# Moving the normed activations by up to 256 bytes within their SBUF tile

## The chip, the cores and the metric

The kernel runs on one core of a Trainium2 chip. The metric is the device time of one execution in microseconds (us). Matmuls run on TensorE (PE; its weight loads are listed apart, as PEld), splits and elementwise work on VectorE (DVE) and ScalarE (ACT), transfers of weights are queued by SyncE (SP), masks are made by GpSimd (POOL).

## The reference

Two transformer blocks over 256 tokens of width 1,024, all in fp32. The first is a mixer (gated delta rule on one half, sliding-window attention on the other) with a SwiGLU FFN; the second is two layers, a short convolution with an FFN and a dilated attention with an FFN. What matters here, cut down:

```python
h = rms_norm(x, norm1_w) * (1.0 + scale1) + shift1      # n = 0
proj = h @ w_in                                         # 11 column blocks, and 16 gate columns
x = x + gate1 * (mixed @ w_out)
h2 = rms_norm(x, norm2_w) * (1.0 + scale2) + shift2     # n = 1
x = x + gate2 * ((silu(h2 @ w_gate) * (h2 @ w_up)) @ w_down)
for i in range(2):                                      # mixers n = 2 and 4, FFNs n = 3 and 5
    h = rms_norm_2(x, mix_norm[i])
    x = x + (short_conv_mixer(h, ...) if i == 0 else dilated_attention_mixer(h, ...))
    h = rms_norm_2(x, ffn_norm[i])
    x = x + swiglu(h, w_gate[i], w_up[i], w_down[i])
```

D_MODEL is 1,024, D_FF 2,816, so that an FFN has eleven blocks of 256 hidden columns.

## The kernel before

**Weights.** They come as 146 blocks of 128 x 2,048 fp32 (1 MB) through a ring of three raw buffers. ACT copies each into a rounded high part (line 585, tiles `w_hi`, `w_hi2`), DVE subtracts it into a low part (line 914, `w_lo`, `w_lo2`). Every product is three matmuls, in this order: high x high, high x low, low x high (the helper `three`, or written out in `gate_up` and `token_rows`). All of them are recorded at line 1474, inside the helper `mm`.

**Normed activations.** Each of the six norms writes its result, split in the same way, into one tile, `h_parts`: the high part, 8 pieces (k) of 256 tokens, 8,192 bytes in each partition, and behind it the low part. `normed(n)` gives the two views for norm n; it starts `H_SHIFT[n]` elements (4 bytes each) into the tile, and `H_ROOM` is the room for it:

```python
H_SHIFT, H_ROOM = (0, 0, 0, 16, 0, 64), 96
h_parts = sb("h_parts", [P, 2 * KD * T + H_ROOM], F32R)
for at in (H_SHIFT[n], H_SHIFT[n] + KD * T)      # in normed(n)
h_hi, h_lo = normed(0)
```

`h_hi` and `h_lo`, the views of norm 0, are used by name in the first mixer, in the column blocks of all mixers and in the writes of norm 1. In the first mixer they hold both the projections' input and later the mixed rows, which four `row_block` calls multiply by `w_out`.

**Places.** Tiles lie one after another in each partition. Between `h_parts` and the weights' tiles before it (`w_hi`, `w_lo`, `x_res`, `norm_tmp`) there are only whole multiples of 256 bytes, and `o_hi`, `o_lo`, `w_hi2`, `w_lo2` lie at the same remainder of 256 too. So at shift 0 all operands of a product start at the weights' remainder; pieces and halves inside them are multiples of 512 bytes on. Shift 16 is 64 bytes further, shift 32 is 128, shift 64 is 256.

**Who moves.** In the FFNs (`gate_up`, n = 1, 3, 5) 128 tokens of h are the stationary operand and gate and up weights, 512 columns, move. Per block j and token half t there are 24 such matmuls; then four transposes of the hidden rows (`turn_hid`, line 1977), their copy to `o_hi` by ACT (line 791) and the split by DVE (line 1347), and 24 matmuls of the down product (`token_rows`) of the block before. Nothing else differs between the three FFNs but the weights, some small products for the modulation and spread rows, and the scale of the norm. In the mixers (`column_half`, `column_block`, `row_block`) 128 columns of the weight are stationary and h moves, 256 tokens wide. The exception is the value block of the dilated attention, where tokens of h are stationary and 256 weight columns move. A product for the gates of the first mixer has only 16 weight columns, 64 bytes per k, as its stationary operand.

**Order.** Each engine's program is one list in a fixed order, tied by semaphores that count (`h_hi_ready`, `h_lo_ready`, `block_used`, `hi_ready`, `lo_ready`); no wait looks at an address.

Of the kernel before, what the change touches and what calls it, by code (L numbers as in the profile page):

```python
# [7 lines left out]
ALU, ACT, AX = mybir.AluOpType, mybir.ActivationFunctionType, mybir.AxisListType  # L8
# [15 lines left out]


WARM_NORM1 = 6
H_SHIFT, H_ROOM = (0, 0, 0, 16, 0, 64), 96
NEXP = 6


# [266 lines left out]
def build(nc, stream, x_in, consts_in, vectors_in, gab_in, t5_onehot, t5_log, rel_bias, out):  # L297
    t5_scratch = nc.dram_tensor("t5_scratch", (16, 384), F32, kind="Internal")
    with ExitStack() as ctx:
        s = Semaphores(lambda name: ctx.enter_context(nc.semaphore(name)))  # L300
# [3 lines left out]
        def sb(name, shape, dt=F32, stack=ctx):  # L304
            return stack.enter_context(nc.sbuf_tensor(name, shape, dt))
# [6 lines left out]
        nt = sb("norm_tmp", [P, KD, T])  # L312
# [20 lines left out]
        def normed(n):  # L333

            return [h_parts[:, at:at + KD * T].rearrange("p (k t) -> p k t", k=KD) for at in (H_SHIFT[n], H_SHIFT[n] + KD * T)]

        h_hi, h_lo = normed(0)
# [100 lines left out]
        def big(name):  # L438
            return BIGB[BIG_INDEX[name] % 3]

        norm_scale = [a1[:, :], a2[:, :], vecs("mix0"), vecs("ffn0"), vecs("mix1"), vecs("ffn1"), vecs("final")]
        shift2 = mods[:, 24:32]
# [121 lines left out]
        def _(act):  # L564
# [38 lines left out]
            def h_high(n, ks=range(KD)):  # L603
                for k in ks:
                    act.wait_ge(s.t_ready, 8 * n + k + 1)
                    if n:
                        act.activation(h_hi[:, k, :], nt[:, k, :], ACT.Identity, bias=shift2[:, k:k + 1]).then_inc(s.h_hi_ready, 1)
                    else:
                        act.activation(h_hi[:, k, :], nt[:, k, :], ACT.Copy).then_inc(s.h_hi_ready, 1)


            act.wait_ge(s.vectors_loaded, 16)
# [14 lines left out]
            for q in range(4):  # L627
                act.activation(high_of(0)[:, 2 * q:2 * q + 2, :], raw_of(r)[:, 2 * q:2 * q + 2, :], ACT.Copy).then_inc(s.first_hi, 1)
                if q == 1:
                    mod_rows_copy(0, 1)  # L630
            hi(1)
            h_high(0, range(4))
            act.dma_start(consts[:, N_FIRST:], consts_in[:, N_FIRST:]).then_inc(s.masks_loaded, 16)
            act.wait_ge(s.gab_loaded, 16)
            act.activation(gab_wh[:, :], gab_w[:, :], ACT.Copy).then_inc(s.gab_hi, 1)
            mod_rows_copy(1, 0)
            mod_rows_copy(1, 1)
            h_high(0, range(4, KD))


# [176 lines left out]
            def ffn(f, following):  # L817

                if f:
                    act.wait_ge(s.rms_ready, 2 * f + 2)  # L820
                else:
                    squares(1)
                    root(1)
                    h_high(1)
# [78 lines left out]
        def _(dve):  # L903
# [74 lines left out]
            def h_parts_2():  # L978
                dve.wait_ge(s.rstd_ready, 2)
                rstd = B[3][:, 256:512]  # L980

                def scaled(k):
                    dve.scalar_tensor_tensor(out=nt[:, k, :], in0=x[:, k, :], scalar=a2[:, k:k + 1],
                                             in1=rstd, op0=ALU.mult, op1=ALU.mult).then_inc(s.t_ready, 1)

                def low(k):
                    dve.wait_ge(s.h_hi_ready, 8 + k + 1)
                    dve.scalar_tensor_tensor(out=h_lo[:, k, :], in0=nt[:, k, :], scalar=shift2[:, k:k + 1],
                                             in1=h_hi[:, k, :], op0=ALU.add, op1=ALU.subtract).then_inc(s.h_lo_ready, 1)

                for k in range(KD):
                    scaled(k)
                    if k >= 1:
                        low(k - 1)
                low(KD - 1)
# [52 lines left out]
            for w in range(6):  # L1048
# [6 lines left out]
                if w < 6:  # L1055
# [9 lines left out]
                    for tap in range(1, 4):  # L1065
                        for mt in range(2):
# [4 lines left out]
                                                           in1=o, op0=ALU.mult, op1=ALU.add)  # L1071
# [6 lines left out]
                if w == 1:  # L1078
# [8 lines left out]
                                             op0=ALU.mult, op1=ALU.min).then_inc(s.gate_dve, 1)  # L1087
                if w == 2:
# [9 lines left out]
                                                  op0=ALU.max, op1=ALU.add))  # L1098
                    dve.scalar_tensor_tensor(out=v8(g[:, :]), in0=v8(gt[:, 6, :]), scalar=-1.0,
                                             in1=gt[:, 4, 0:8].unsqueeze(1).broadcast_to([P, TT, 8]),  # L1100
                                             op0=ALU.mult, op1=ALU.mult).then_inc(s.gate_done, 1)
# [79 lines left out]
            for gi in range(4):  # L1181
# [6 lines left out]
                                                    op0=ALU.mult, op1=ALU.mult))  # L1188
            for i, name in enumerate(("sq01", "sq23")):
                wait_big(name)  # L1190
                big_read(name, dve.scalar_tensor_tensor(out=qs[:, 2 * i:2 * i + 2, :], in0=qs[:, 2 * i:2 * i + 2, :],
                                                        scalar=qk_w[:, :], in1=two(big(name)), op0=ALU.mult, op1=ALU.mult))
# [187 lines left out]
            for i in range(4):  # L1380
# [14 lines left out]
                for tap in range(3):  # L1395
                    for mt in range(2):
# [5 lines left out]
                        else:  # L1402
                            link(dve.scalar_tensor_tensor(out=yb[:, mt, :], in0=cu[:, mt, tap:tap + T], scalar=vec[:, ck:ck + 1],
                                                          in1=yb[:, mt, :], op0=ALU.mult, op1=ALU.add))
# [805 lines left out]
```

## Time and profile before

| | |
|---|---|
| median of 3 runs | 1070.27 us (1069.92 to 1070.87) |
| the profiled execution | 1070.55 us, its span 1068.8 us |
| PE busy | 1033.9 us, 97% |
| DVE busy | 618.6 us, 58% |
| ACT busy | 481.0 us, 45% |
| mean granted TensorE clock | 0.981 |

Busy time is the union of the instructions' recorded times. Matmuls are pipelined, so the recorded time of one (some 390 ns for 512 columns) is longer than the distance to the next; the distance comes from start times in the timeline. A timeline row with `x2` is two instructions of one kind in a row, and its time is that of both. What lies outside the span (1.75 us) is not in the trace.

### The profile page before, as it was taken

The page shows a single profiled execution, that of the slowest core. Times are in us where ns is not written, and L with a number is a line of the kernel's source. Part 1 is how long each engine was busy: PE and PEld are TensorE (multiplying, and loading weights), DVE is VectorE, ACT ScalarE, POOL GpSimd, SP SyncE. Part 2 cuts the span into 40 slices and gives each one's busy share as a digit, 9 for nine tenths or more (in the row PEclk, how much of TensorE's full clock was granted, in tenths as well). Part 3 has the DMA queues.
Part 4 walks back from the last instruction along what each step waited for, and adds up shares of the span by engine and source line. Part 5 has one row for each costly group of instructions (what it writes and reads, how often), then busy time and mean ns, then how long its engine had stood idle before and what let it go on. Part 6 is the DMA issues. An engine that isn't in the chain of part 4 may idle for free.

```text
span 1068.8 us, 14676 instructions
## 1 busy us (share of the span) xinstructions
PE 1033.9 (97%) x6224; PEld 898.3 (84%) x6224; DVE 618.6 (58%) x753; ACT 481.0 (45%) x644; POOL 49.5 (5%) x43
## 2 busy tenths in 40 slices
PE   6999979999999999999999999999999999999997
PEld 3799979989788788889987888888899978888885
DVE  1586575866646553568765545454677555454543
ACT  2475443523634434453426434344555465344342
POOL 0000353400000000000000000000000000000000
PEclk9999987989999999999999999999999999999998
DMA  9645004463856653536545364554453326554621
GB/s 346 255 166 184 1 2 158 156 238 131 293 207 236 236 215 140 207 109 237 197 158 191 132 229 155 199 186 175 172 178 119 119 99 215 199 197 157 235 80 39
DMA packets 31552, 185.63 MB, mean 174 GB/s; under 512 B 3008, under 2 KB 5504, under 8 KB 10752
## 3 DMA queue, kind: packets, MB, share of 16 engines
q1 hardware_dynamic: 29952, 180.37, 46.9%
q0 software_dynamic: 832, 3.17, 0.9%
q8 instruction: 49, 0.80, 0.3%
q10 hardware_dynamic: 704, 1.17, 0.3%
q14 instruction: 15, 0.12, 0.0%
HBM read 183.62 MB, written 1.07 MB: 173 GB/s over the span
## 4 chain that ended last, share of the span: by engine, by line
PE 85%; DVE 6%; ACT 4%; DMA 3%; issue 2%; POOL 0%; SPq 0%; ACTq 0%; DVEq 0%; POOLq 0%
PE bank L1474 44%; PE acc L1474 37%; DVE w_lo L914 2%; ACT w_hi L585 2%; DMA raw<-stream 2%; PE bank L1977 1%; DMA AT<-stream 1%; ACT norm_tmp L713 1%; PE bank L1871 1%; DVE soft L1207 1%; PE bank L1817 0%; DVE XT L1183 0%; DVE norm_tmp L1200 0%; PE acc L1567 0%; ACT L786 0%
## 5 line engine op out<-in xcount | busy, mean ns | idle before, releaser
L914 DVE TENSOR_TENSOR w_lo<-raw,w_hi 128x2048 fp32r<-128x2048 f32 x145 | 331.7, 2304 | 162.0 <-ACT w_hi L585 161.8
L1474 PE MATMUL bank<-w_hi,h_parts 128*128 128x512 f32 x1056 | 336.8, 393 | 3.4 <-DVE w_lo L914 3.4
L585 ACT ACTIVATE w_hi<-raw 128x2048 fp32r<-128x2048 f32 x145 | 272.9, 1908 | 98.2 <-PE acc L1474 63.2
L1474 PEld LDWEIGHTS bank<-w_hi,h_parts 128*128 128x128 f32 x1056 | 198.9, 188 | 48.6 <-DVE w_lo L914 4.7
L1474 PE MATMUL bank<-w_lo,h_parts 128*128 128x512 f32 x528 | 207.0, 392 | 0.0
L1474 PE MATMUL acc<-h_parts,w_hi 128*128 128x256 f32 x928 | 173.7, 289 | 0.0
L1474 PEld LDWEIGHTS acc<-h_parts,w_hi 128*128 128x128 f32 x928 | 147.5, 196 | 2.6 <-issue 2.1
L1474 PE MATMUL acc<-h_parts,w_lo 128*128 128x256 f32 x464 | 132.7, 286 | 0.0
L1474 PE MATMUL acc<-w_hi,o_hi 128*128 128x512 f32 x296 | 119.0, 402 | 0.0
L1474 PEld LDWEIGHTS bank<-w_lo,h_parts 128*128 128x128 f32 x528 | 99.5, 188 | 21.1
L1474 PE MATMUL acc<-w_hi,o_lo 128*128 128x512 f32 x296 | 115.7, 391 | 0.0
L1474 PE MATMUL acc<-w_lo,o_hi 128*128 128x512 f32 x296 | 115.6, 391 | 0.0
L1474 PEld LDWEIGHTS acc<-h_parts,w_lo 128*128 128x128 f32 x464 | 90.7, 195 | 0.0
L786 ACT ACTIVATE silu_and_hid<-bank,rms 128x256 f32<-128x256 f32 x44 | 20.9, 476 | 107.3 <-PE bank L1474 107.2
L1347 DVE TENSOR_TENSOR o_lo<-bank,o_hi 128x512 fp32r<-128x512 f32 x33 | 22.8, 692 | 79.7 <-ACT o_hi L791 79.4
L1474 PEld LDWEIGHTS acc<-w_hi,o_lo 128*128 128x128 f32 x296 | 55.6, 188 | 12.3
L1474 PEld LDWEIGHTS acc<-w_hi,o_hi 128*128 128x128 f32 x296 | 55.6, 188 | 11.1 <-issue 0.2
L1474 PEld LDWEIGHTS acc<-w_lo,o_hi 128*128 128x128 f32 x296 | 55.7, 188 | 10.7
L791 ACT ACTIVATE o_hi<-bank 128x512 fp32r<-128x512 f32 x33 | 19.8, 599 | 77.6 <-PE bank L1977 77.6
L1339 DVE SCALAR_TENSOR_TENSOR silu_and_hid<-bank,rms,silu_and_hid 128x256 f32<-128x256 f32 x44 | 21.2, 481 | 34.4 <-ACT silu_and_hid L786 34.4
L550 POOL TENSOR_TENSOR inv_b<-AT,consts 128x512 f32<-128x512 f32 x24 | 35.4, 1502 | 34.2 <-PE bank L1474 34.2
L1474 PE MATMUL bank<-h_parts,w_hi 128*128 128x256 f32 x192 | 34.9, 284 | 0.0
(324 smaller groups left out, 1093.9 us busy)
## 6 DMA issues: line engine op xcount, KB each, us to landing
raw<-stream SPq DMA_DIRECT2D x162, 1024.0 KB, 5.0
AT<-stream SPq DMA_DIRECT2D x2, 1024.0 KB, 11.2
qkT<-stream SPq DMA_DIRECT2D x2, 1024.0 KB, 9.3
X_inv<-stream SPq DMA_DIRECT2D x2, 1024.0 KB, 10.0
keys_queries<-stream SPq DMA_DIRECT2D x2, 1024.0 KB, 10.5
t_tables<-t_scratch POOLq DMA_DIRECT2D x1, 2048.0 KB, 11.8
x_res<-x_in SPq DMA_DIRECT2D x2, 512.0 KB, 5.3
t_tables<-t_scratch POOLq DMA_DIRECT2D x1, 1024.0 KB, 14.1
```

The costliest lines, as they stand in the source:

```text
L550: pool.tensor_tensor(Bm[:, gi, :].rearrange("p (i c) -> p i c", i=4), AT[:, gi, :].rearrange("p (i c) -> p i c", i=4), level_mask[l].unsqu ...
L585: act.activation(high_of(w), raw_of(r), ACT.Copy).then_inc(s.hi_ready, 1)
L713: act.activation(sc[:, hh, c0:c1], sc[:, hh, c0:c1], ACT.Exp, bias=soft[:, 1, 2 * hh + part:2 * hh + part + 1], accum_out=soft[:, 2, 2 * h ...
L786: act.activation(sg[:, T * t:T * t + T], B[t][:, 0:256], ACT.Silu, scale=rms[:, t:t + 1] if f else 1.0).then_inc(s.silu_ready, 1)
L791: act.activation(hid_parts(j)[0].rearrange("p a b -> p (a b)"), B[2][:, :], ACT.Copy).then_inc(s.hid_hi_ready, 1)
L914: dve.tensor_tensor(low_of(w), raw_of(weight_load(w)), high_of(w), ALU.subtract).then_inc(s.lo_ready, 1)
L1207: link(dve.tensor_reduce(soft[:, 0, 2 * hh + part:2 * hh + part + 1], sc[:, hh, c0:c1], AX.X, ALU.max))
L1339: dve.scalar_tensor_tensor(out=o, in0=up, scalar=rms[:, t:t + 1], in1=gate, op0=ALU.mult, op1=ALU.mult).then_inc(s.hid_ready, 1)
L1347: dve.tensor_tensor(low.rearrange("p a b -> p (a b)"), B[2][:, :], high.rearrange("p a b -> p (a b)"), ALU.subtract).then_inc(s.hid_lo_rea ...
L1474: return pe.matmul(o, l, r, start=start, stop=stop, skip_group_check=True)
L1871: ins = pe.transpose(B[gi][:, c], X[:, gi, c], ident)
L1977: ins = pe.transpose(B[2][:, T * i + P * t:T * i + P * t + P], hid[:, T * t + P * i:T * t + P * i + P], ident)
```

## The change

The shifts of the six norms go from (0, 0, 0, 16, 0, 64) elements to (32, 0, 32, 0, 32, 0). The FFNs' h (n = 1, 3, 5) then starts at the weights' remainder, the mixers' h (n = 0, 2, 4) 128 bytes on. Since `h_hi` and `h_lo` stay the views of norm 0, they move with the mixers, and the writes of norm 1 are given the views of their own norm.

```diff
-H_SHIFT, H_ROOM = (0, 0, 0, 16, 0, 64), 96
+H_SHIFT, H_ROOM = (32, 0, 32, 0, 32, 0), 96
...
                     if n:
-                        act.activation(h_hi[:, k, :], nt[:, k, :], ACT.Identity, bias=shift2[:, k:k + 1]).then_inc(s.h_hi_ready, 1)
+                        act.activation(normed(n)[0][:, k, :], nt[:, k, :], ACT.Identity, bias=shift2[:, k:k + 1]).then_inc(s.h_hi_ready, 1)
                     else:
-                        act.activation(h_hi[:, k, :], nt[:, k, :], ACT.Copy).then_inc(s.h_hi_ready, 1)
+                        act.activation(normed(n)[0][:, k, :], nt[:, k, :], ACT.Copy).then_inc(s.h_hi_ready, 1)
...
                     dve.wait_ge(s.h_hi_ready, 8 + k + 1)
-                    dve.scalar_tensor_tensor(out=h_lo[:, k, :], in0=nt[:, k, :], scalar=shift2[:, k:k + 1],
-                                             in1=h_hi[:, k, :], op0=ALU.add, op1=ALU.subtract).then_inc(s.h_lo_ready, 1)
+                    dve.scalar_tensor_tensor(out=normed(1)[1][:, k, :], in0=nt[:, k, :], scalar=shift2[:, k:k + 1],
+                                             in1=normed(1)[0][:, k, :], op0=ALU.add, op1=ALU.subtract).then_inc(s.h_lo_ready, 1)
```

## Rows read from the trace of the kernel before

**Rows 1.** The page: busy time of each engine, and the chain that ended last by line.

```profile
PE 1033.9 (97%) x6224; PEld 898.3 (84%) x6224; DVE 618.6 (58%) x753; ACT 481.0 (45%) x644; POOL 49.5 (5%) x43
...
PE bank L1474 44%; PE acc L1474 37%; DVE w_lo L914 2%; ACT w_hi L585 2%; DMA raw<-stream 2%; PE bank L1977 1%; DMA AT<-stream 1%; ACT norm_tmp L713 1%; PE bank L1871 1%; DVE soft L1207 1%; PE bank L1817 0%; DVE XT L1183 0%; DVE norm_tmp L1200 0%; PE acc L1567 0%; ACT L786 0%
```

**Rows 2.** The list of the tile h_parts: duration min/median/max in ns, first and last start.

```profile
L1474 PE MATMUL bank<-w_hi,h_parts x1056: 387/389/628, 269.3 to 1047.0; 128*128 128x512 f32 x176
...
L1474 PE MATMUL acc<-h_parts,w_hi x928: 277/283/580, 34.1 to 831.9; 128*128 128x256 f32 x186
...
L1474 PE MATMUL bank<-h_parts,w_hi x192: 277/283/363, 465.5 to 519.4; 128*128 128x256 f32 x192
...
L1474 PE MATMUL acc<-w_hi,h_parts x128: 279/283/286, 764.6 to 837.8; 128*128 128x256 f32 x128
...
L810 ACT ACTIVATE h_parts<-bank,vec x16: 465/476/485, 464.0 to 868.6; 128x256 fp32r<-128x256 f32 x16
```

**Rows 3.** Timeline of PE, second FFN, a gate/up product: start us, us, instruction.

```profile
598.95 0.63 PE L1474 MATMUL bank<-w_hi,h_parts 128*128 128x512 f32 x2
...
601.05 0.63 PE L1474 MATMUL bank<-w_hi,h_parts 128*128 128x512 f32 x2
```

**Rows 4.** Timeline of PE, third FFN, a gate/up product.

```profile
920.66 0.62 PE L1474 MATMUL bank<-w_hi,h_parts 128*128 128x512 f32 x2
...
922.70 0.62 PE L1474 MATMUL bank<-w_hi,h_parts 128*128 128x512 f32 x2
```

**Rows 5.** Timeline of ACT, second FFN: line 791 in its third and eighth block.

```profile
605.37 0.60 ACT L791 ACTIVATE o_hi<-bank 128x512 fp32r<-128x512 f32 x1 [2.71 <-PE bank L1977]
...
691.18 0.60 ACT L791 ACTIVATE o_hi<-bank 128x512 fp32r<-128x512 f32 x1 [2.71 <-PE bank L1977]
```

**Rows 6.** Timeline of ACT, third FFN: line 791 in the same two blocks.

```profile
914.23 0.60 ACT L791 ACTIVATE o_hi<-bank 128x512 fp32r<-128x512 f32 x1 [2.68 <-PE bank L1977]
...
998.30 0.60 ACT L791 ACTIVATE o_hi<-bank 128x512 fp32r<-128x512 f32 x1 [2.68 <-PE bank L1977]
```

**Rows 7.** Timeline of PE, first FFN, behind an interruption.

```profile
290.82 0.63 PE L1474 MATMUL bank<-w_hi,h_parts 128*128 128x512 f32 x2
...
292.90 0.62 PE L1474 MATMUL bank<-w_hi,h_parts 128*128 128x512 f32 x2
...
294.94 0.39 PE L1474 MATMUL bank<-w_hi,h_parts 128*128 128x512 f32 x1
```

**Rows 8.** Windows: second FFN, third FFN, conv mixer; busy us (count), PEclk, DMA share, GB/s.

```profile
605.00:691.00 86.00, 86.00 (x385) 69.79 (x383) 41.80 (x30) 35.42 (x30) 0.00 (x0) 1.00 0.51 184
914.00:998.00 84.00, 84.00 (x382) 69.46 (x381) 41.78 (x30) 35.37 (x30) 0.00 (x0) 1.00 0.52 187
464.00:548.00 84.00, 83.27 (x646) 80.82 (x645) 64.34 (x75) 36.47 (x38) 0.00 (x0) 1.00 0.50 174
```

**Rows 9.** Timeline of PE, conv mixer, a column product.

```profile
480.03 0.40 PE L1474 MATMUL bank<-h_parts,w_hi 128*128 128x256 f32 x2
...
481.83 0.40 PE L1474 MATMUL bank<-h_parts,w_hi 128*128 128x256 f32 x2
```

**Rows 10.** Timeline of PE, first projections, behind a restart at 56.12 us.

```profile
56.46 0.28 PE L1474 MATMUL acc<-h_parts,w_lo 128*128 128x256 f32 x1
...
57.90 0.28 PE L1474 MATMUL acc<-h_parts,w_lo 128*128 128x256 f32 x1
```

**Rows 11.** Timeline of PE, the gate product of 16 weight columns.

```profile
49.62 0.39 PE L1474 MATMUL bank<-h_parts,gab_wh 128*16 128x256 f32 x2
...
51.66 0.39 PE L1474 MATMUL bank<-h_parts,gab_wh 128*16 128x256 f32 x2
```

**Rows 12.** Timeline of PE, attention, around an idle stretch.

```profile
770.28 0.28 PE L1474 MATMUL acc<-w_hi,h_parts 128*128 128x256 f32 x1
772.53 2.63 PE L1474 MATMUL bank<-x_res 64*128 64x256 f32 x16 [1.97 <-DVE x_res L1437]
```

**Rows 13.** Window right behind that stretch; columns as in Rows 8.

```profile
773.00:776.00 3.00, 3.00 (x20) 2.75 (x17) 2.37 (x2) 2.08 (x4) 0.00 (x0) 0.51 0.98 371
```

## The prediction

> **What bounds the kernel now.** I read the page first: the matmuls are busy 97% of the span, and the chain that ended last is 85% PE, with line 1474, the one through which nearly every product goes, at 44% and 37% [rows 1]. DVE and ACT are at 58% and 45%. So the pace at which PE starts its matmuls sets the time. The second view, the list of the tile that the change moves, says how many of them read it [rows 2]. Its rows with the high weight hold two of every three products, so the total is one and a half times the count: 1,056 x 1.5 = 1,584 matmuls with 512 columns in the three FFNs (there h is the stationary operand), (928 + 192) x 1.5 = 1,680 with 256 columns where h is the moving one, and 128 x 1.5 = 192 more, in the value blocks of the attention, where h is stationary again and a weight of 256 columns moves. Busy times are no pace, because matmuls overlap; I took paces from start times in the timeline.
>
> **The pace by the place of h.** The three FFNs run the same code. Before, h stands at shift 0 in the first, 64 bytes on in the second, 256 bytes on in the third. The reader should count nine matmuls in each timeline: in the second FFN from 598.95 to 601.05 us, 2.10 us or 233.3 ns each [rows 3]; in the third from 920.66 to 922.70, 2.04 us or 226.7 ns each [rows 4]. The copy of the turned hidden rows (line 791) comes once per FFN block and gives the whole block: (691.18 - 605.37) / 5 = 17.16 us in the second [rows 5], (998.30 - 914.23) / 5 = 16.81 in the third [rows 6]. The first FFN, at shift 0, settles at the third's pace, nine in 292.90 to 294.94 us or 226.7 ns each [rows 7]. So 256 bytes further is no different from none, and 64 bytes further costs 0.35 us per block. 48 gate/up matmuls by 6.6 ns are 0.32 of it; the remaining 0.03 is the start of the down product, which leaves the slow rhythm after a few matmuls.
>
> **The change, part by part.** (1) Third FFN, from 256 bytes to 0: the same remainder, so nothing (first FFN against third above). (2) First FFN: stays at 0. Its writes go through another name, with the same address. (3) Second FFN, from 64 bytes to 0: its eleven blocks should go at the third's pace, 11 x 0.348 = **-3.8 us**. Nothing else holds them: the third FFN does the same loads and splits at that pace, with DVE busy 41.8 of 84 us and DMA at 0.52 [rows 8]. (4) The writes of h: ACT's take 465 to 485 ns over all the places that h has now [rows 2], and DVE's follow them, so nothing. (5) Waits: none is added or taken away, the semaphores and every instruction's place in its queue stay. (6) The three mixers, from 0 to 128 bytes: this is the unknown. They start a matmul every 120.0 ns: fifteen from 480.03 to 481.83 us [rows 9]. That is the conv mixer; the first projections show the same, twelve from 56.46 to 57.90 us [rows 10]. No row has a full 128-column weight load against a 256-column moving operand half a period away.
>
> **The bounds of part 6.** Below: the gate products load only 16 columns, from an operand whose remainder goes on by 64 bytes with each k, and start every 113.3 ns, eighteen in 49.62 to 51.66 us, with no difference between the k [rows 11]. So 113.3 is what 256 moving columns reach here when hardly any weight load runs beside them. The 120.0 is one step of 6.7 ns over that, and the FFN's 64 bytes are one step of the same size. One step down over 1,680 + 192 = 1,872 matmuls is at most -12.5 us; I allow a tenth for places where PE waits for others, so -11.3. Above: one step up, as the 64 bytes did, 1,872 x 6.7 = +12.5 us, with nothing to hide it because PE is already the bound (83.3 of 84 us in the conv mixer [rows 8]). Which value? After an interruption the two streams of PE, loads and matmuls, stand to each other in another way before they settle. In the FFN that costs visibly: nine matmuls from 290.82 to 292.90 take 2.08 us, 231 ns each, before the 226.7 [rows 7]. In the projections the twelve of rows 10 are the ones right behind a restart (at 56.12 us), and they already take 120.0 each on average. So with 256 columns the pace hardly depends on how the two streams stand to each other, at 512 it does. That is nearest to no change, and I take **0** for part 6, with both ends kept.
>
> The Trainium skill (SBUF — State Buffer, "Who interferes with whom") gives TensorE two independent read ports, one for the moving operand and one for the weight load, and says that PE never waits on anyone. By that rule no shift would matter and the sum would be 0, that is 1070.3 us; the 17.16 against 16.81 us per block speaks against it.
>
> The skill also gives a start-to-start time of N / 2.4 GHz + about 2.5 ns for warm bf16 matmuls (TensorE: Matmul & The Clock Gate, "Wait — 56ns, not 53.3ns?"): 109.2 ns for 256 columns. By that the mixers would have 10.8 ns each to give back, an estimated 20 us over 1,872; no row here reaches it.
>
> **The sum.** The profiled execution took 1070.55 us, 1068.8 of it span; the median of the runs is 1070.27, 0.3 less. 1070.55 - 3.8 = 1066.7, and against the median **1066.5**.
>
> **The rivals.**
> *Mixers faster.* If half a period keeps the two streams apart, the pace goes one step down, to 113.3. For it: the step exists [rows 11]. Against: 113.3 is seen only with a load an eighth as long, and a load of 128 columns may need the rest whatever its address. Time: 1070.3 - 3.8 - 11.3 = 1055.
> *Mixers slower (the other side).* The moving stream of one matmul and the load for the next both begin at the same time; at equal remainders they are in step, and an offset made them collide more once, in the second FFN. If 128 bytes do the same as 64, every mixer matmul takes 126.7. For it: the only shifted stage of before is the slow one. Against: there the offset was 64, on the other operand, with 512 columns; and the restarts of the mixers show no slower phase. Time: 1070.3 - 3.8 + 12.5 = 1079. It decides from 3.8 / 1,872 = 2.1 ns per matmul on: above that the kernel is slower than before.
> *Nothing changes.* The second FFN's slower blocks would have to come from something other than the address. Its ACT and DVE work is the same as the third's (35.4 and 41.8 us in five blocks [rows 8]), so little speaks for it. Time: 1070.3.
> *The clock.* PE stands idle for 1.97 us before 772.53 us in the attention [rows 12], and the granted clock is 0.51 from 773 to 776 us, the lower of its two levels; earlier starts could move such a stretch over more or less work [rows 13]. That is 1 to 2 us either way, no case of its own.
>
> **How the numbers follow.** Chances: second FFN gains and the mixers keep their pace (to within about 1 ns) 0.45, with its own range 1065 to 1068.1; mixers faster 0.27; mixers slower 0.23; nothing changes 0.05. About 0.2% (2.1 us) is what a measurement can tell from no change, so "faster" begins at 1068.1. Faster: 0.43 + 0.27 = 0.70. Same: 0.02 of the first case, 0.05 of nothing, 0.03 of mixers slightly slower = 0.10. Slower: 0.20. The range goes from 1054, just past the faster rival, to 1073, which takes in mixers slower by up to 3.5 ns; what lies outside is most of the slower rival and a few hundredths below.
>
> **What would show it.** In the profile after: line 791 of the second FFN every 16.81 us instead of 17.16 (part 3); the first and third FFN unchanged at 16.8 (parts 1, 2); three column matmuls of the conv mixer in 0.36 us (part 6 at 0), 0.34 (faster) or 0.38 (slower), and the length of that stage, 84 us, with it. The prediction is wrong if the mixers' pace moves by over 1 ns per matmul, since there are 1,872 of them, or if the second FFN keeps 17.16.

## The result, and the profile after

The changed kernel takes 1060.22 us (median of 9 runs, 1057.87 to 1062.30), the one before, in runs beside it and the three shown above, 1066.44 us. The ratio is 0.9937, 95% interval 0.9914 to 0.9959: faster, by 6.7 us (4.4 to 9.2). One execution of the kernel before took 3542.74 us, as one of e3_mix_only did later with 4737.13; both are left out of the ratios. The 6.7 us lean on the three runs of before shown above (1069.92 to 1070.87): against the other five, which average 1064.7 us, the changed kernel's average of 1060.1 is 4.7 us less. Two later series of the same kernel against the one before gave 0.9949 (0.9928 to 0.9971) and 0.9944 (0.9924 to 0.9964), 5.4 and 6.0 us. Forecast were 3.8 us.

The page after, the lines that answer to [rows 1]; the picture is the same, PE 97% busy and 84% of the chain:

```profile
PE 1023.1 (97%) x6224; PEld 892.2 (84%) x6224; DVE 618.4 (58%) x753; ACT 480.7 (45%) x644; POOL 49.1 (5%) x43
...
PE bank L1474 44%; PE acc L1474 36%; DVE w_lo L914 2%; ACT w_hi L585 2%; DMA raw<-stream 2%; PE bank L1977 1%; DMA AT<-stream 1%; ACT norm_tmp L713 1%; PE bank L1871 1%; DVE soft L1207 1%; PE bank L1817 0%; DVE XT L1183 0%; DVE h_parts L1318 0%; DVE norm_tmp L1200 0%; ACT L786 0%
```

Line 791 in the second FFN after, the blocks of [rows 5] (timeline of ACT):

```profile
599.31 0.60 ACT L791 ACTIVATE o_hi<-bank 128x512 fp32r<-128x512 f32 x1 [2.68 <-PE bank L1977]
...
683.38 0.60 ACT L791 ACTIVATE o_hi<-bank 128x512 fp32r<-128x512 f32 x1 [2.68 <-PE bank L1977]
```

(683.38 - 599.31) / 5 = 16.81 us per block instead of 17.16, and the third FFN has (988.94 - 904.87) / 5 = 16.81 as before:

```profile
904.87 0.60 ACT L791 ACTIVATE o_hi<-bank 128x512 fp32r<-128x512 f32 x1 [2.68 <-PE bank L1977]
...
988.94 0.60 ACT L791 ACTIVATE o_hi<-bank 128x512 fp32r<-128x512 f32 x1 [2.68 <-PE bank L1977]
```

Nine gate/up matmuls of the second FFN, as in [rows 3], take 2.04 us, 226.7 ns each instead of 233.3 (timeline of PE):

```profile
593.00 0.62 PE L1474 MATMUL bank<-w_hi,h_parts 128*128 128x512 f32 x2
...
595.04 0.62 PE L1474 MATMUL bank<-w_hi,h_parts 128*128 128x512 f32 x2
```

The mixers, where h now moves 128 bytes off. Paces below are worked out from rows rounded to 0.01 us, so that two of them over 33 matmuls that differ by 0.3 ns can be one and the same, and where a range is given it is of averages over 24 matmuls. In the first projections 33 matmuls lie between these two rows (timeline of PE), 3.91 us or 118.5 ns each, where [rows 10] had 120.0:

```profile
63.90 0.40 PE L1474 MATMUL acc<-h_parts,w_hi 128*128 128x256 f32 x2
...
67.81 0.40 PE L1474 MATMUL acc<-h_parts,w_hi 128*128 128x256 f32 x2
```

In the conv mixer of the same execution 30 matmuls take 3.59 us, 119.7 ns each, near the 120.0 of [rows 9]:

```profile
479.99 0.40 PE L1474 MATMUL acc<-h_parts,w_hi 128*128 128x256 f32 x2
...
483.58 0.40 PE L1474 MATMUL acc<-h_parts,w_hi 128*128 128x256 f32 x2
```

The gate product of [rows 11], with its load of 16 columns, went the other way: 18 matmuls take 2.10 us, 116.7 ns each instead of 113.3.

```profile
44.78 0.39 PE L1474 MATMUL bank<-h_parts,gab_wh 128*16 128x256 f32 x2
...
46.88 0.40 PE L1474 MATMUL bank<-h_parts,gab_wh 128*16 128x256 f32 x2
```

**Where the two profiled executions differ.** The spans are 1068.8 and 1059.2 us, 9.6 apart, more than the ratio says. Line 657, ACT's first copy of a projection, shows why (its list: duration, first and last start). First before, then after:

```profile
L657 ACT ACTIVATE inv_p<-acc x6: 580/598/602, 49.5 to 80.6; 128x512 f32<-128x512 f32 x6
```

```profile
L657 ACT ACTIVATE inv_p<-acc x6: 577/602/603, 45.0 to 76.1; 128x512 f32<-128x512 f32 x6
```

The kernel's start is 4.5 us shorter after, though the change has no hold on it: only 74 matmuls that read h are recorded ahead of that copy, 0.1 us at 1.5 ns each. The timeline of PE says it. Before, three matmuls of 256 columns are 0.64 us apart (34.06 to 34.70), the pace of the lower clock level, and 0.35 from 35.89 on:

```profile
34.06 0.63 PE L1474 MATMUL acc<-h_parts,w_hi 128*128 128x256 f32 x2
...
34.70 0.63 PE L1474 MATMUL acc<-h_parts,w_hi 128*128 128x256 f32 x2
...
35.89 0.40 PE L1474 MATMUL acc<-h_parts,w_hi 128*128 128x256 f32 x2
...
36.24 0.40 PE L1474 MATMUL acc<-h_parts,w_hi 128*128 128x256 f32 x2
```

After, they are at the fast pace from the first (31.09 to 31.45), because the clock had risen before they began:

```profile
31.09 0.40 PE L1474 MATMUL acc<-h_parts,w_hi 128*128 128x256 f32 x2
...
31.45 0.40 PE L1474 MATMUL acc<-h_parts,w_hi 128*128 128x256 f32 x2
```

That is a matter of the execution, not of the kernel: e4_scan and e5_mix64 below are the same program up to there, with h of norm 0 at the same 64 bytes, and have the copy at 44.5 and 49.3 us. Among the later profiles three began late as well (line 657 first at 49.5 us in e2_ffn_only, 49.3 in e5_mix64, 49.2 in e8_scan2), the others had it at 44.4 to 47.1. The three runs of before from which the prediction started (1070.27 us) lie at the upper end of what this kernel does: its median was 1064.8 to 1066.0 in three later series of 14 to 21 runs, from 1063.4 to 1070.7. I therefore compare stretches behind the start-up: the first projections (line 657's first copy to line 696), the conv mixer (line 791's last in the first FFN to its first in the second), the second FFN (its first 791 to its last), and the attention (to the third FFN's first). All in us:

| kernel | shifts of mixers, FFNs (bytes) | projections | conv mixer | second FFN | attention |
|---|---|---|---|---|---|
| before | 0; 0, 64, 256 | 73.85 | 123.38 | 163.25 | 146.09 |
| e2_ffn_only | 0; 0 | 73.86 | 123.26 | 159.99 | 146.11 |
| e3_mix_only | 128; 0, 64, 256 | 73.39 | 122.62 | 163.26 | 145.38 |
| after | 128; 0 | 73.48 | 123.25 | 159.99 | 145.57 |
| e1_after | 128; 0 | 73.49 | 122.54 | 159.99 | 145.43 |
| e12_after_again | 128; 0 | 73.39 | 122.51 | 159.99 | 145.39 |
| e5_mix64 | 64; 0 | 72.93 | 121.75 | 159.95 | 142.77 |
| e10_mix176 | 176; 0 | 73.63 | 122.90 | 159.99 | 145.60 |
| e6_mix192 | 192; 0 | 71.52 | 121.99 | 159.95 | 141.54 |
| e11_mix192_again | 192; 0 | 71.51 | 122.00 | 159.99 | 143.18 |
| e9_mix208 | 208; 0 | 73.49 | 121.56 | 159.99 | 145.22 |

### The profile page after: what moved, and what is told of

It reads as the page before. It is cut to its first block, busy times and chain, and to the rows that moved or that the text cites. A ratio compares the mean times of both kernels' runs of the same rounds, so it can differ in the third digit from the quotient of the medians.

```text
span 1059.2 us, 14676 instructions
## 1 busy us (share of the span) xinstructions
PE 1023.1 (97%) x6224; PEld 892.2 (84%) x6224; DVE 618.4 (58%) x753; ACT 480.7 (45%) x644; POOL 49.1 (5%) x43
## 4 chain that ended last, share of the span: by engine, by line
PE 84%; DVE 7%; ACT 4%; DMA 3%; issue 2%; POOL 0%; SPq 0%; ACTq 0%; DVEq 0%; POOLq 0%
PE bank L1474 44%; PE acc L1474 36%; DVE w_lo L914 2%; ACT w_hi L585 2%; DMA raw<-stream 2%; PE bank L1977 1%; DMA AT<-stream 1%; ACT norm_tmp L713 1%; PE bank L1871 1%; DVE soft L1207 1%; PE bank L1817 0%; DVE XT L1183 0%; DVE h_parts L1318 0%; DVE norm_tmp L1200 0%; ACT L786 0%
## 5 line engine op out<-in xcount | busy, mean ns | idle before, releaser
L1474 PEld LDWEIGHTS acc<-h_parts,w_hi 128*128 128x128 f32 x928 | 145.0, 192 | 3.8 <-issue 3.4
L1474 PE MATMUL acc<-w_hi,o_hi 128*128 128x512 f32 x296 | 119.0, 402 | 0.0
```

What stands on the lines that cost most here:

```text
L1474: return pe.matmul(o, l, r, start=start, stop=stop, skip_group_check=True)
```

## The experiments

### The changed kernel twice more

No edit. Beside it ran the two kernels that follow.

> The changed kernel once more, five rounds against the kernel before on one chip. Theory A (the address alone, in the second FFN 0.348 us for each of eleven blocks, in the first projections and the attention about 1 ns per matmul): 4 to 5 us less than before, ratio 0.9955 to 0.9965. Rival B (the first result is all of it, something beyond the matmul paces gives 2 to 3 us more): 6.5 us less, ratio 0.994. Rival C (the moment at which the clock first rises in the start-up differs from run to run, and makes 4 to 5 us of spread in both kernels alike): the ratio goes toward A's, and the profile shows the first fast matmuls at a place of its own, between about 23 and 36 us.

Measured: 1060.97 us, ratio 0.9949 (0.9928 to 0.9971), with the sums of its stretches at -0.36, -0.84, -3.26 and -0.66 against before. The start-up account (C) and the stage account (A) hold together. The interval does not exclude 0.994, so B is not refuted by the ratio; but the stretches behind the start leave 2 to 3 us more no place. Line 657 comes first at 45.6 us here, an early start like that of the first profile.

> The changed kernel again. The sum of the stages in the traces so far is 3.4 us from the second FFN and 1.4 to 2.1 from the mixers: 4.8 to 5.5 us less than before, ratio 0.9948 to 0.9955. The conv mixer at 118.7 or at 120.0 ns.

Measured: 1060.66 us, ratio 0.9944 (0.9924 to 0.9964), which takes in the forecast 0.9948 to 0.9955; the conv mixer at 118.8 ns: 33 matmuls in 3.92 us (timeline of PE).

```profile
479.83 0.40 PE L1474 MATMUL bank<-h_parts,w_hi 128*128 128x256 f32 x2
...
483.75 0.40 PE L1474 MATMUL acc<-h_parts,w_hi 128*128 128x256 f32 x2
```

So the conv mixer of the same kernel has 118.5 and 118.8 ns in two profiles and 119.7 in the first, with 0.7 us between the stretches (123.25 against 122.54 and 122.51). The same place gives one of two rhythms. They also come in one execution: in the attention of the changed kernel most matmuls are at 118.6 ns, but those from 767 to 777 us are at 120.0.

### Only the FFNs, only the mixers

```diff
-H_SHIFT, H_ROOM = (32, 0, 32, 0, 32, 0), 96
+H_SHIFT, H_ROOM = (0, 0, 0, 0, 0, 0), 96
```

> Only the FFN part of the change: all six norms at shift 0, mixers as before. Theory A: line 791 of the second FFN every 16.81 us, mixers at 120.0 ns as before, 3.8 us less than before in all (ratio 0.9964). If the mixers' 128 bytes are worth more than 1 us, this one stays behind the changed kernel by that much; if 128 bytes cost something, it is faster than the changed kernel.

Measured: 1061.22 us, ratio 0.9955 (0.9934 to 0.9976). Line 791 of the second FFN comes at (688.88 - 604.80) / 5 = 16.82 us, and no mixer stretch moves by over 0.12 us against before:

```profile
604.80 0.60 ACT L791 ACTIVATE o_hi<-bank 128x512 fp32r<-128x512 f32 x1 [2.68 <-PE bank L1977]
...
688.88 0.60 ACT L791 ACTIVATE o_hi<-bank 128x512 fp32r<-128x512 f32 x1 [2.68 <-PE bank L1977]
```

The second FFN gives 163.25 - 159.99 = 3.26 us, its first product, which lies in the stretch before, 0.12: 3.4 us in all. The ratio alone can't part the FFN from the mixers: this kernel's interval overlaps those of both later series of the changed kernel. The stretches can.

```diff
-H_SHIFT, H_ROOM = (32, 0, 32, 0, 32, 0), 96
+H_SHIFT, H_ROOM = (32, 0, 32, 16, 32, 64), 96
```

> Only the mixer part: norms 0, 2, 4 at 128 bytes, the second FFN still at 64 and the third at 256 bytes. Theory A: line 791 of the second FFN stays at 17.16 us; first projections at about 118.7 ns per matmul instead of 120.0, conv mixer 120.0; 0.5 to 1.5 us less than before, hardly to be told from no change (ratio 0.9985 to 0.9995). Rival B: 2 to 3 us less (ratio 0.9975).

Measured: 1063.57 us, ratio 0.9975 (0.9959 to 0.9990). The second FFN stays at (685.02 - 599.21) / 5 = 17.16:

```profile
599.21 0.60 ACT L791 ACTIVATE o_hi<-bank 128x512 fp32r<-128x512 f32 x1 [2.71 <-PE bank L1977]
...
685.02 0.60 ACT L791 ACTIVATE o_hi<-bank 128x512 fp32r<-128x512 f32 x1 [2.71 <-PE bank L1977]
```

The interval lies below 1, but part of that may be the start-up, since none of these runs is among the late ones of 1066 to 1071 us that the kernel before has. The stretches show what the 128 bytes of the mixers are worth by themselves, in the conv mixer too, which was expected to stay at 120.0 ns: 0.46 in the projections, 0.76 in the conv mixer, 0.71 in the attention, 1.9 us together, and 0.3 behind the projections, where the clock also moves. With the FFN's 3.4 that makes 5.3 to 5.7, beside the 5.4 and 6.0 that the two later series of the changed kernel gave.

### Other places of h

To give each norm a place of its own, the column products of the second and third mixer, and the value block of the third, read their own norm's views:

```diff
-H_SHIFT, H_ROOM = (32, 0, 32, 0, 32, 0), 96
+H_SHIFT, H_ROOM = (16, 32, 48, 48, 8, 8), 96
...
-                    ins = three(bank[:, 256 * mt:256 * mt + 256], wh[:, k, c], wl[:, k, c], h_hi[:, k, :], h_lo[:, k, :],
+                    ins = three(bank[:, 256 * mt:256 * mt + 256], wh[:, k, c], wl[:, k, c], normed(views)[0][:, k, :], normed(views)[1][:, k, :],
```

> A look at six other places of h: norm 0 at 64 bytes, norm 2 at 192, norm 4 at 32 (h moves, 256 columns), norm 1 at 128, norm 3 at 192, norm 5 at 32 (h stationary, 512 columns move). If the cost goes in steps of 6.7 ns with the distance in bytes modulo 256, the FFN paces are 226.7, 233.3 or 240 ns and FFN blocks 16.8, 17.16 or 17.5 us. If only equal remainders are good, all three FFNs are at 17.1 us or above. If h moving with 256 columns is indifferent, the mixers stay between 118 and 121 ns at all three places.

Measured: 1062.37 us, one run, like those of the next two kernels. The moving h had 117.8 ns at 64 bytes (projections) and at 192 (conv mixer) and mostly 116.7 to 118.2 at 32 (attention): it is not indifferent. Stationary, in the second FFN at 192 bytes, 12 matmuls take 2.74 us, 228.3 ns each, and in the third at 32 bytes 12 take 2.80, 233.3 (timelines of PE):

```profile
592.09 0.62 PE L1474 MATMUL bank<-w_hi,h_parts 128*128 128x512 f32 x2
...
594.83 0.62 PE L1474 MATMUL bank<-w_hi,h_parts 128*128 128x512 f32 x2
```

```profile
896.65 0.63 PE L1474 MATMUL bank<-w_hi,h_parts 128*128 128x512 f32 x2
...
899.45 0.63 PE L1474 MATMUL bank<-w_hi,h_parts 128*128 128x512 f32 x2
```

> A second look at six places of h: norm 0 at 96 bytes, norm 2 at 160, norm 4 at 224 (moving), norm 1 at 16, norm 3 at 224, norm 5 at 160 (stationary). From the first look: h stationary at 0 has 226.7 ns, at 32, 64, 128 and 192 bytes 233.8, 233.4, 232.2 and 229. If the distance counts by itself and grows gently toward 256 again, 224 bytes is near 227 to 228, 160 near 230 to 231, and 16 between 226.7 and 233.8. For h moving 117 to 118.7 everywhere off 0, so that only equal remainders (120.0) are the poor case.

The edit was the same with (24, 4, 40, 56, 56, 40). Measured: 1071.76 us, in an execution whose start was late. The forecast for h moving fell at 96 bytes, where the projections have 120.0 ns, as at 0 (33 matmuls in 3.96 us; timeline of PE):

```profile
63.23 0.40 PE L1474 MATMUL acc<-h_parts,w_hi 128*128 128x256 f32 x2
...
67.19 0.40 PE L1474 MATMUL acc<-h_parts,w_hi 128*128 128x256 f32 x2
```

At 160 bytes the conv mixer has 117.2 to 118.8 ns, at 224 the attention's column products have 117.8 to 118.7. The FFN block per place of the stationary h, from line 791 in these two profiles and those above:

| bytes off the weights' remainder | 0 | 16 | 32 | 64 | 128 | 160 | 192 | 224 |
|---|---|---|---|---|---|---|---|---|
| us per FFN block | 16.81 | 16.80 | 17.14 | 17.16 | 17.07 | 17.18 | 16.92 | 17.14 |

Not a gentle function of the distance: 224 bytes, which I had expected near 227 ns, is as bad as 32 (17.14), while 192 is nearly good. Neither "steps of 6.7 ns" nor "only equal remainders are good" describes it; 0 is the best place for the stationary h, shared by 16. The entries for 16 and 128 bytes rest on two blocks each: they are the first FFN's, most of whose blocks are longer for other reasons (17.2 us and more at 0 too).

### One common move of all operands

```diff
-        sb("spacer_before", [P, 24])
+        sb("spacer_before", [P, 32])
```

> The changed kernel with the spacer before the weights' tiles 128 instead of 96 bytes: all places relative to each other stay, the weights' own remainder of 256 goes from 224 to 0. Theory A (only the distance between stationary and moving operand counts): paces as in the changed kernel, 226.7 ns in the FFNs, 118.6 to 120.0 in the mixers, 113.3 for the gate product. Rival (the 6.7 ns over 106.7 of the gate product are those of an operand that doesn't start at a multiple of 64 bytes, one more line to read): one step less everywhere, 220, 112 to 113 and 107 to 109 ns, which over all matmuls would be 20 us.

Measured: 1062.73 us. The weights' tiles, h and everything behind them move by 32 bytes, the raw blocks don't. 226.7 ns in the FFN (15 matmuls in 3.40 us) and 118.8 in the projections (33 in 3.92), where the changed kernel had 226.7 and 118.5 (timelines of PE); its conv mixer had 120.0, one of the two rhythms of this place:

```profile
593.64 0.61 PE L1474 MATMUL bank<-w_hi,h_parts 128*128 128x512 f32 x2
...
597.04 0.61 PE L1474 MATMUL bank<-w_hi,h_parts 128*128 128x512 f32 x2
```

```profile
63.92 0.40 PE L1474 MATMUL acc<-h_parts,w_hi 128*128 128x256 f32 x2
...
67.84 0.40 PE L1474 MATMUL acc<-h_parts,w_hi 128*128 128x256 f32 x2
```

This common move changes nothing; others weren't tried. The gate product has 116.7 ns, not the 113.3 expected, but so has the changed kernel: for it, too, the distance to h counts. The account by operands that don't start at 64 bytes is out, since no pace went down a step.

### The mixers elsewhere

```diff
-H_SHIFT, H_ROOM = (32, 0, 32, 0, 32, 0), 96
+H_SHIFT, H_ROOM = (16, 0, 16, 0, 16, 0), 96
```

and likewise with 48, 44 and 52 elements.

> FFNs at shift 0 as in the changed kernel, the three mixers at 64 bytes instead of 128. The look at other places gave 117.6 ns per matmul for the first projections there, against 118.6 to 120.0 at 128 bytes. Theory A (the pace at a place belongs to the place, in every mixer): 117.6 ns in the first projections, the conv mixer and the attention, 1 to 2.4 ns times 1,872 = 2 to 4.5 us less than the changed kernel, ratio to before 0.991 to 0.9935. Rival: the pace belongs to the stage (which buffers of the weights, which work beside it), and only the first projections gain: 0.5 us less than the changed kernel.

> The same with the mixers at 192 bytes, where the look gave 117.8 ns in the conv mixer. Theory A: 117.6 to 117.8 ns in all three mixers, no difference from the 64 bytes that the ratio can tell, 1.5 to 4 us less than the changed kernel. If 128 bytes were the best place of those three, both this and the 64 bytes would be slower than the changed kernel.

At 64 bytes 1057.52 us, ratio 0.9939 (0.9911 to 0.9968); at 192 bytes 1056.00 us, ratio 0.9908 (0.9880 to 0.9937). At 192 the 33 matmuls of the projections take 3.74 us, and so do 33 in the attention: 113.3 ns each.

```profile
63.92 0.39 PE L1474 MATMUL acc<-h_parts,w_hi 128*128 128x256 f32 x2
...
67.66 0.39 PE L1474 MATMUL acc<-h_parts,w_hi 128*128 128x256 f32 x2
```

```profile
768.04 0.39 PE L1474 MATMUL acc<-h_parts,w_hi 128*128 128x256 f32 x2
...
771.78 0.39 PE L1474 MATMUL acc<-h_parts,w_hi 128*128 128x256 f32 x2
```

In its conv mixer they take 3.89 us, 117.9 ns each:

```profile
477.96 0.40 PE L1474 MATMUL acc<-h_parts,w_hi 128*128 128x256 f32 x2
...
481.85 0.40 PE L1474 MATMUL acc<-h_parts,w_hi 128*128 128x256 f32 x2
```

So a full weight load of 128 columns fits beside 256 moving ones in 113.3 ns; it depends on the place, and on something more, since the conv mixer doesn't reach it at the same place.

The profile at 64 bytes shows what that is not. Its projections are at 117.8 ns throughout, but its conv mixer starts at 113.3 (33 matmuls in 3.74 us) and goes on at 117.8 (33 in 3.88, by these rows 117.6). The change comes in the middle of its second column block, behind the small product of the norm (`bank<-consts,rms`) that stands there. The attention does the same at the same point, and two of its four value blocks have 113.3 (timeline of PE):

```profile
471.21 0.39 PE L1474 MATMUL bank<-h_parts,w_hi 128*128 128x256 f32 x2
...
474.95 0.39 PE L1474 MATMUL bank<-h_parts,w_hi 128*128 128x256 f32 x2
...
475.29 0.60 PE L1474 MATMUL bank<-consts,rms 128*128 128x128 f32 x4
...
476.09 0.40 PE L1474 MATMUL bank<-h_parts,w_hi 128*128 128x256 f32 x2
...
479.97 0.40 PE L1474 MATMUL bank<-h_parts,w_hi 128*128 128x256 f32 x2
```

At 192 bytes, too, some stretches of the projections are at 117.8 ns (from 78 to 92 us). So 64 and 192 bytes have the same two paces, and differ in which of them most of the matmuls have. Theory A in its strict form (one pace per place) falls, and so does the rival of e5 (only the projections gain): the pace can change within a stage. The attention at 64 bytes (142.77 us) is 2.6 us shorter than in the changed kernel, but some 1.6 of it is the clock, as the next run shows.

> Mixers at 192 bytes once more, beside the changed kernel on one chip. If the pace belongs to the place alone: 113.3 ns in the first projections and the attention and 117.8 in the conv mixer again, ratio to before about 0.991. If each execution falls into one of several rhythms (the conv mixer of the changed kernel had 120.0 in one profile and 118.7 in another), the conv mixer may be at 113.3 this time or the others at 117 to 118, and the ratio goes with it, between 0.9905 and 0.994.

Measured: 1056.40 us, ratio 0.9907 (0.9886 to 0.9929), beside the changed kernel's 0.9944 on the same chip. The conv mixer has 117.9 ns again (33 matmuls in 3.89 us).

The attention was 1.64 us shorter the first time (141.54 against 143.18). The sixteen score products behind the idle stretch of [rows 12] took 1.68 us there and 2.67 here, with the same 2.12 us of idle time before them (timelines of PE, e6 and then e11):

```profile
760.18 1.68 PE L1474 MATMUL bank<-x_res 64*128 64x256 f32 x16 [2.12 <-DVE x_res L1437]
```

```profile
759.85 2.67 PE L1474 MATMUL bank<-x_res 64*128 64x256 f32 x16 [2.12 <-DVE x_res L1437]
```

The granted clock behind it was 1.00 in the one and 0.50, the lower level, in the other (windows; columns as in [rows 8]):

```profile
761.00:763.00 2.00, 2.00 (x20) 1.88 (x19) 1.81 (x1) 1.48 (x4) 0.00 (x0) 1.00 0.86 352
```

```profile
761.00:763.00 2.00, 2.00 (x12) 1.78 (x10) 2.00 (x1) 1.60 (x3) 0.00 (x0) 0.50 0.97 401
```

The same idle stretch costs the lower clock in one execution and not in the next; of the profiles taken, e4_scan, e5_mix64 and e6_mix192 didn't pay it, all the others did.

> FFNs at 0, mixers at 176 bytes, the other neighbour of 192. 160 bytes gave 118.5 in the conv mixer. The same two cases: 117 to 119 ns if 192 stands alone, 113 to 115 if it doesn't.

> FFNs at 0, mixers at 208 bytes. So far h moving takes 120.0 ns per matmul at 0 bytes, 118.7 or 120.0 at 128, 117 to 118 at 32 and 64, 113.3 (first projections, attention) and 117.8 (conv mixer) at 192. If 192 is a single good place, 208 is back at 117 to 119; if it is the edge of a good stretch, 113 to 115 ns.

At 176 bytes 1061.22 us, ratio 0.9954 (0.9935 to 0.9973), at 208 bytes 1058.56 us, ratio 0.9926 (0.9903 to 0.9949). The projections have 119.4 ns (33 in 3.94 us) and 119.0 (30 in 3.57; timeline of PE):

```profile
64.05 0.40 PE L1474 MATMUL acc<-h_parts,w_hi 128*128 128x256 f32 x2
...
67.62 0.40 PE L1474 MATMUL acc<-h_parts,w_hi 128*128 128x256 f32 x2
```

In the projections and the attention 192 bytes stands alone among its neighbours. In the conv mixer it doesn't: at 208 bytes 33 matmuls take 3.85 us, 116.7 ns each, and the stretch of 121.56 us is the shortest of all, shorter than the 122.0 at 192. Neither expected case had that.

```profile
480.05 0.40 PE L1474 MATMUL acc<-h_parts,w_hi 128*128 128x256 f32 x2
...
483.90 0.39 PE L1474 MATMUL acc<-h_parts,w_hi 128*128 128x256 f32 x2
```

The kernel with the FFNs at 0 and the mixers at 192 bytes is the best that ran: its two intervals, 0.9880 to 0.9937 and 0.9886 to 0.9929, overlap the changed kernel's, but the stretches are shorter in each profile, by 2.0 us in the projections, 0.5 to 1.3 in the conv mixer and 2.2 in the attention where both had the low clock behind the idle stretch.

## Why the prediction was right in kind and short in size

**Third and first FFN, nothing (parts 1, 2): right.** The third FFN's stretch from its first 791 to its last is 161.84 us before and after, the first FFN's 165.49 and 165.43.

**Second FFN, -3.8 us (part 3): right in mechanism, 0.4 us too large.** The block went from 17.16 to 16.81 exactly. But I took eleven of them. The first two copies of line 791 lie only 8.8 us apart (8.78 before, 8.65 after), since that stretch holds one gate/up product and no down product, and the first product of all runs behind a restart, in no settled rhythm (0.12 us). e2_ffn_only gives 3.4.

**Writes and waits, nothing (parts 4, 5): right.** No stretch outside the products moved in e2_ffn_only.

**Mixers, 0 (part 6): wrong by 0.9 to 1.9 us in the three stretches** (three profiles of the changed kernel against e2_ffn_only), and by some tenths more behind the projections. This is the term that was off. By the prediction's own sign (over 1 ns per matmul) it was wrong: most mixer matmuls went from 120.0 to 118.6 ns. The sentence "with 256 columns the pace hardly depends on how the two streams stand to each other" was drawn from twelve matmuls behind a restart that average 120.0 ns. At 128 bytes the pace is mostly 118.5 to 119 ns in the projections and the attention of every profile, and in the conv mixer of three out of five; the other two have 120 there; at 64 it is mostly 117.8, at 192 mostly 113.3. Behind a restart the addresses are still the same; what differs is the time between the streams, and that says little of another distance in bytes. The sentence fails as it stands as well: at 64 bytes a small product in between took the pace from 113.3 to 117.8 ns.

**The faster rival** (0.27, 1055 us) did not come in at 128 bytes. Its objection, that 113.3 was seen only beside a load of 16 columns and that a full load may need the rest, was refuted at 64 and 192 bytes, where the full step down exists. The floor itself was read at one place of h: at 128 bytes the gate product has 116.7. And the load of 16 columns is an eighth in columns, not in time: it is recorded with 94 ns, one of 128 columns with 192. **The slower rival** did not come in anywhere: no place off 0 was slower than 120.0 in a settled mixer, though 96 bytes had 120.0 and a projection stretch of 73.95 us against 73.85 before. That 64 bytes cost the stationary h a step and give the moving h 2.2 ns shows that the loss of one could not be carried over to the other. **Nothing changes** was out with the first block, and with it the forecast drawn from what the Trainium skill says of independent read ports (SBUF — State Buffer, "Who interferes with whom"): the projections go from 120.0 to 113.3 ns by the place of h alone (before and e6_mix192). Whether it is the ports at which the two operands meet is not shown. The Trainium skill's N / 2.4 GHz + about 2.5 ns, measured there with bf16 (TensorE: Matmul & The Clock Gate, "Wait — 56ns, not 53.3ns?"), would be 109.2; the best place leaves 113.3.

**The base.** 1066.5 was worked out from 1070.27; with the later series' 1064.8 to 1066.0 the same sum gives 1061 to 1062.2, against a measured 1060.2 to 1061.0. The forecast of 1066.5 was 6.3 us off, mostly by this; that the range from 1054 to 1073 held the result owes something to its width, which was set by the two rivals. The clock was named as good for 1 to 2 us; in the start-up, where I had not looked, it is worth 4.5.

## What to carry to other kernels

Where matmuls follow each other without a gap, read the distance between their starts, not their durations, and compare stages that run the same code with operands at other distances modulo 256 bytes: here that alone gave the FFN term within 0.4 us. The distance between stationary and moving operand is worth a sweep for each form of product (16 and 32 byte steps, one profile can hold six places), since neither form's best place nor the sign of an offset carries over to the other. Look at the whole stage for it: one place can have two paces, and a few matmuls show only one. Take effects of a few us from stretches of the trace behind the start-up, where the moment of the clock's rise can hide them.

## What the runs showed of the hardware that was not expected

A settled stream of 256-column matmuls with a weight load each has several paces at 1.00 granted clock: 113.3, 116.7, 117.8, 118.6, 119.0 to 119.4, 120.0 ns. Which ones can come up depends on the distance of the operands (of the ten that ran, 113.3 came up at 64 and 192 bytes alone), and one distance can have two: 113.3 and 117.8 at 64 and 192, 118.6 and 120.0 at 128, 116.7 and 119.2 at 208. In e5_mix64 the pace changed within one column block, behind a small product that came between, with the same h and the same buffers; so what comes just before has a hand in it, and not only the place or the stage. What decides which of the two it is, and so why the conv mixer stays at 117.8 at 192 bytes, is open: no experiment changed the start of a stretch alone.

With 512 moving columns the block times of eight places jump (0 and 16 bytes 16.8 us, 192 bytes 16.92, 128 bytes 17.07, 32, 64, 160 and 224 bytes 17.14 to 17.18). I have no mechanism that gives these numbers and none was tested; only that a common move of both operands by 32 bytes changes nothing is shown.

The window view gives a granted clock of 1.00 for a stretch of the start-up in which the matmuls run at the lower level's pace (before, 213 ns for 256 columns at 34.06 us); the record begins with the rise at about 35.8 us:

```profile
30.00:34.00 4.00, 4.00 (x13) 3.48 (x14) 2.27 (x8) 2.65 (x4) 0.00 (x0) 1.00 1.09 402
```
